# A one-core decoder block in float32: shared squares of x, a shorter sum of h, a second operand of w_o in halves, and a residual that is added in PSUM

## The reference

```
h      = rmsnorm(x, attn_norm_g)
proj   = h @ w_in            # conv B, C, x (1024 each), q 1024, k 128, v 128, two gates (1024 each)
y_conv = (u_b * short_conv(u_c * u_x)) @ w_conv_out          # causal, 3 taps
attn   = softmax over a window of 128 keys, with a position bias and a sink logit per head
mixed  = sigmoid(g_conv) * y_conv + sigmoid(g_attn) * (attn @ w_attn_out)
x      = x + mixed @ w_o
x      = x + square(relu(rmsnorm(x, mlp_norm_g) @ w_up)) @ w_down      # hidden 4096
out    = rmsnorm(x, final_norm_g)
```

## Time and profile before

| | us |
|---|---|
| median of 3 runs | 751.18 |
| the profiled execution | 751.2 |
| its span in the trace | 749.5 |
| PE busy (matmuls) | 741.1 (99%) |
| DVE busy | 656.3 (88%) |
| ACT busy | 430.0 (57%) |
| POOL busy | 85.5 (11%) |

### The profile page before, as it was taken

One profiled execution on the slowest core, in us unless ns is written; L12 is line 12 of the kernel. 1 busy time (PEld: TensorE's weight loads), 2 busy tenths in 40 slices (PEclk: granted clock), 3 DMA queues, 4 the chain that ended last, 5 costly groups with the idle time before them and its releaser, 6 DMA issues.

```text
span 749.5 us, 10670 instructions
## 1 busy us (share of the span) xinstructions
PE 741.1 (99%) x4198; PEld 650.7 (87%) x4198; DVE 656.3 (88%) x759; ACT 430.0 (57%) x551; POOL 85.5 (11%) x120
## 2 busy tenths in 40 slices
PE   9999999999999999999999999999999999999996
PEld 8899888888888888888888899889988999899985
DVE  5996788989899686989999999998799879986997
ACT  6773555453644557564658776654565455545555
POOL 1520000111122101010100101010101010100102
PEclk9999999999999999999999999999999999999999
DMA  9899313161247987777767747677677767686703
GB/s 319 200 316 321 112 57 113 57 164 61 84 127 236 305 232 196 195 225 193 255 169 177 213 124 208 179 201 193 169 191 202 174 171 219 168 215 180 197 1 113
DMA packets 69443, 135.45 MB, mean 181 GB/s; under 512 B 2636, under 2 KB 18068, under 8 KB 69396
## 3 DMA queue, kind: packets, MB, share of 16 engines
q1 hardware_dynamic: 48848, 85.23, 33.6%
q0 software_dynamic: 20336, 49.30, 30.3%
q10 hardware_dynamic: 212, 0.28, 0.1%
HBM read 128.48 MB, written 6.32 MB: 180 GB/s over the span
## 4 chain that ended last, share of the span: by engine, by line
PE 94%; DVE 4%; ACT 1%; issue 1%; POOL 0%; POOLq 0%; DVEq 0%; ACTq 0%
PE pair L1085 45%; PE pair L1044 22%; PE pair L790 6%; PE pair L792 6%; PE pair L791 6%; PE pair L911 3%; PE pair L837 2%; PE pair L812 1%; PE pair L811 1%; PE pair L821 1%; PE pair L859 1%; DVE h L1788 1%; PE pair L1007 0%; PE pair L995 0%; DVE wgt L1745 0%
## 5 line engine op out<-in xcount | busy, mean ns | idle before, releaser
L1390 ACT ACTIVATE high<-home_raw 128x2048 fp32r<-128x2048 f32 x91 | 174.3, 1916 | 148.4 <-PE pair L1085 102.9
L2014 DVE TENSOR_TENSOR home_lo<-home_raw,high 128x2048 fp32r<-128x2048 f32 x91 | 208.4, 2290 | 34.6 <-ACT high L1390 34.1
L1085 PE MATMUL pair<-high,s_hi_tile 128*128 128x512 f32 x440 | 110.3, 391 | 0.3 <-ACT s_hi_tile L1472 0.3
L1085 PE MATMUL pair<-high,s_lo_tile 128*128 128x512 f32 x440 | 109.9, 390 | 0.0
L1085 PE MATMUL pair<-home_lo,s_hi_tile 128*128 128x512 f32 x440 | 109.5, 389 | 0.0
L1085 PEld LDWEIGHTS pair<-home_lo,s_hi_tile 128*128 128x128 f32 x440 | 82.5, 188 | 17.1
L1085 PEld LDWEIGHTS pair<-high,s_lo_tile 128*128 128x128 f32 x440 | 82.4, 188 | 17.1
L1085 PEld LDWEIGHTS pair<-high,s_hi_tile 128*128 128x128 f32 x440 | 81.8, 188 | 17.7 <-issue 0.7
L790 PE MATMUL pair<-h,wgt 128*128 128x512 f32 x192 | 76.5, 399 | 0.0
L792 PE MATMUL pair<-h,wgt 128*128 128x512 f32 x192 | 75.0, 390 | 0.0
L791 PE MATMUL pair<-h,wgt 128*128 128x512 f32 x192 | 74.9, 390 | 0.0
(11 more groups left out here) (228 smaller groups left out, 1129.5 us busy)
## 6 DMA issues: line engine op xcount, KB each, us to landing
home_raw<-in_w_up SPq DMA_DIRECT2D x16, 1024.0 KB, 5.3
home_raw<-in_w_down SPq DMA_DIRECT2D x16, 1024.0 KB, 5.1
raw<-in_w_in SPq DMA_DIRECT2D x26, 512.0 KB, 4.8
home_raw<-in_w_up POOLq DMA_DIRECT2D x12, 1024.0 KB, 8.2
home_raw<-in_w_down POOLq DMA_DIRECT2D x12, 1024.0 KB, 8.4
home_raw<-in_w_in POOLq DMA_DIRECT2D x7, 1024.0 KB, 8.6
home_raw<-in_w_in SPq DMA_DIRECT2D x7, 1024.0 KB, 7.1
home_raw<-in_w_conv_out SPq DMA_DIRECT2D x4, 1024.0 KB, 5.2
```

Of the source, the lines that this page charges most:

```text
L1085: last = mm(pair[region(s, i)][:, b, :], a_[:, k, b * P:(b + 1) * P], w[:, k, :], start=(fresh and kind == 0 and k == 0), stop=(kind == 2 ...
L1390: a(high[n % 2][:, :], home_raw[home_of(s, name)][:, :], ACT.Copy).then_inc(m_hi, 1)
L2014: v.tensor_tensor(home_lo[home][:, :], home_raw[home][:, :], f32(high[n % 2][:, :]), ALU.subtract).then_inc(m_lo, 1)
```

## The change

Four places are touched.

**Squares of x.** For rows 0, ACT squares columns 0 to 511 only, and for rows 1 columns 0 to 767; DVE does the rest by a multiply with accumulation (`share_of_squares`), which leaves sum/1024 + 1e-6 in `share`. The root takes `share` as its bias instead of the constant. Both DVE pieces stand ahead of both `scale_x` on DVE, and rows 1 are scaled ahead of the copy of the parameters (`pcol`). On ACT `root(2)` moves ahead of the four copies of h's tiles.

**One h sum.** S1 = h11 + S2, computed in two steps from the split parts, becomes A - B from the two unsplit blocks in `qa`: one DVE instruction of 128 x 1024 for two. `hs_step` has one step fewer, and the copies that overwrite `qa` wait for step 4 instead of 3.

**w_o's second operand in halves.** ACT's high copy for N2 of stage WO becomes two of 128 x 512; TensorE's first two matmuls wait for the first (`o_first`), the third for the second.

**Last rows' residual in PSUM.** Ahead of the last product, DVE adds `res` of rows 3 into the accumulator in PSUM (`add_residual`), and TensorE waits for it (`rested`) before N4. The last `drain_n4` goes; ACT sums the squares and DVE scales straight from PSUM.

```diff
+SQUARED = (D // 2, 3 * D // 4, D, D)
...
+                            if s == WO and i == N2:
+                                pe.wait_ge(o_first, 1)
+                            elif s >= CO:
...
+                        if s == WO and i == N2 and (b, kind, k) == (0, 0, 2):
+                            pe.wait_ge(s_hi, part_no(s, i) + 1)
...
                 pe.wait_ge(drained, base_ + 4 + more)
+                if s == STAGES - 1:
+                    pe.wait_ge(rested, 1)
...
                 act.wait_ge(x_in[b], 16)
-                a(ta[:, :, :].rearrange("p a n -> p (a n)"), xn[:, b, :], ACT.Square,
+                n = SQUARED[b]
+                a(ta[:, :, :].rearrange("p a n -> p (a n)")[:, 0:n], xn[:, b, 0:n], ACT.Square,
                   accum_out=ssq[:, b:b + 1]).then_inc(sq_done, 1)
                 act.wait_ge(sq_done, b + 1)
-                a(rms[:, 0, b:b + 1], ssq[:, b:b + 1], ACT.Sqrt, bias=eps[:, :], scale=1.0 / D).then_inc(root_done, 1)
+                if n < D:
+                    act.wait_ge(share_done, b + 1)
+                a(rms[:, 0, b:b + 1], ssq[:, b:b + 1], ACT.Sqrt, bias=share[:, b:b + 1] if n < D else eps[:, :],
+                  scale=1.0 / D).then_inc(root_done, 1)
...
             q_high_half(M1, 1)
+            root(2)
             act.wait_ge(par_ready, 1)
...
-            root(2)
             q_high_half(N2, 0)
...
-                act.wait_ge(hs_step, {M7: 2, M6: 3, M5: 5, M3: 7}[i])
+                act.wait_ge(hs_step, {M7: 2, M6: 3, M5: 4, M3: 6}[i])
...
+                if (s, i) == (WO, N2):
+                    first = 2
+                    a(s_hi_tile[slot_of(s, i)][:, 0:2, :], src[:, 0:2, :], ACT.Copy).then_inc(o_first, 1)
+                a(s_hi_tile[slot_of(s, i)][:, first:4, :], src[:, first:4, :], ACT.Copy).then_inc(s_hi, 1)
...
-                act.wait_ge(drained, drained_before(STAGES - 1) + 6 + b)
+                if b < 3:
+                    act.wait_ge(drained, drained_before(STAGES - 1) + 6 + b)
+                else:
+                    wait_used(act, STAGES - 1, N4)
...
+            def share_of_squares(b):
+
+                n = D - SQUARED[b]
+                dve.wait_ge(x_in[b], 16)
+                v.tensor_tensor_reduce(out=ty[:, b, 0:n], in0=xn[:, b, D - n:D], in1=xn[:, b, D - n:D], scale=1.0 / D,
+                                       scalar=EPS, op0=ALU.mult, op1=ALU.add, accum_out=share[:, b:b + 1]
+                                       ).then_inc(share_done, 1)
...
+            share_of_squares(0)
+            share_of_squares(1)
             scale_x(0)
+            scale_x(1)
             dve.wait_ge(par_t, 1)
             v.tensor_copy(pcol[:, :], bank[KT - 1][:, T - 5 * KT:T]).then_inc(par_ready, 1)
-            scale_x(1)
...
             def h_s1():
-                step_done(3)
-                v.tensor_tensor(hs_sum[2][:, :, :], h_part(0, 0, 0), hs_sum[1][:, :, :], ALU.add).then_inc(hs_step, 1)
-                step_done(4)
-                v.tensor_tensor(hs_sum[2][:, :, :], hs_sum[2][:, :, :], h_part(1, 0, 0), ALU.add).then_inc(hs_step, 1)
+                v.tensor_tensor(hs_sum[2][:, :, :], four_of(qa, 1, 0), four_of(qa, 1, 1), ALU.subtract).then_inc(hs_step, 1)
...
+            def add_residual():
+
+                s = STAGES - 1
+                dve.wait_ge(drained, drained_before(s) + 5)
+                acc = pair[region(s, N4)][:, 1, :]
+                v.tensor_tensor(acc, acc, res[:, 3, 0:512], ALU.add).then_inc(rested, 1)
...
+                src = pair[region(STAGES - 1, N4)][:, 1, :] if b == 3 else r
...
                 if last:
+                    add_residual()
                     drain_last_m3(0)
...
             gain(3)
-            drain_n4(STAGES - 1, 1)
             factor(2)
```

More of the change, by code:

```diff
@@ L319, in build @@
         ssq = place("ssq", [P, TB])
+        share = place("share", [P, 2])
         rms = place("rms", [P, 2, TB])
@@ L364, in build @@
         h_hi, h_ready = sem("h_hi"), sem("h_ready")
-        wide = sem("wide")
+        wide, share_done = sem("wide"), sem("share_done")
         q_b11, q_b21 = ([sem(f"{n}{e}") for e in range(2)] for n in ("q_b11_", "q_b21_"))
@@ L393, in build @@
         copied, half_copied = sem("copied"), sem("half_copied")
-        o_seeded = sem("o_seeded")
+        o_seeded, o_first = sem("o_seeded"), sem("o_first")
         summed, relu_done = sem("summed"), sem("relu_done")
@@ L397, in build @@
         ao_sum = sem("ao_sum")
-        prod, drained, gfin_in = sem("prod"), sem("drained"), sem("gfin_in")
+        prod, drained, rested, gfin_in = sem("prod"), sem("drained"), sem("rested"), sem("gfin_in")
         passed = sem("passed")
@@ L1073, in product @@
                             pe.wait_ge(m_hi, n + 1)
-                            if s >= CO:
+                            if s == WO and i == N2:
+                                pe.wait_ge(o_first, 1)
+                            elif s >= CO:
                                 pe.wait_ge(s_hi, part_no(s, i) + 1)
@@ L1309, in q_copy @@
                 if i:
-                    act.wait_ge(hs_step, 3)
+                    act.wait_ge(hs_step, 4)
                 a(four_of(qa, i, j), four(Q_REGION.get(of, 3))[:, :, :], ACT.Copy, scale=scale).then_inc(done, 1)
@@ L1470, in s_high @@
                 wait_used(act, *part_before(s, i))
-                src = four(0) if (s, i) == (WO, N2) else part_source(s, i)
-                a(s_hi_tile[slot_of(s, i)][:, :, :], src[:, :, :], ACT.Copy).then_inc(s_hi, 1)
+                src, first = four(0) if (s, i) == (WO, N2) else part_source(s, i), 0
+                if (s, i) == (WO, N2):
+                    first = 2
+                    a(s_hi_tile[slot_of(s, i)][:, 0:2, :], src[:, 0:2, :], ACT.Copy).then_inc(o_first, 1)
+                a(s_hi_tile[slot_of(s, i)][:, first:4, :], src[:, first:4, :], ACT.Copy).then_inc(s_hi, 1)
             def seed(s):
@@ L1611, in square, with last_rows @@
                 a(a_part(s, i, j), src[:, :, :], ACT.Square).then_inc(squared, 1)
+            def last_rows(b, ch):
+                return pair[region(STAGES - 1, N4)][:, 1, :] if (b, ch) == (3, 0) else res[:, b, 512 * ch:512 * ch + 512]
             def sum_squares(b, ch, part):
-                a(tz[:, 0, 0:512], res[:, b, 512 * ch:512 * ch + 512], ACT.Square,
+                src = last_rows(b, ch) if part else res[:, b, 512 * ch:512 * ch + 512]
+                a(tz[:, 0, 0:512], src, ACT.Square,
                   accum_out=ss3[:, part, b:b + 1]).then_inc(ss3_ready, 1)
@@ L1846, in h_s4 @@
                 v.tensor_tensor(hs_sum[3][:, :, :], h_part(0, 0, 1), hs_sum[1][:, :, :], ALU.add).then_inc(hs_step, 1)
-                step_done(6)
+                step_done(5)
                 v.tensor_tensor(hs_sum[3][:, :, :], hs_sum[3][:, :, :], h_part(1, 0, 1), ALU.add).then_inc(hs_step, 1)
@@ L2375, in scale_late @@
                 r = res[:, b, 512 * ch:512 * ch + 512]
-                v.scalar_tensor_tensor(out=r, in0=r, scalar=rms3[:, 2, b:b + 1], in1=gfin[:, 512 * ch:512 * ch + 512],
+                src = pair[region(STAGES - 1, N4)][:, 1, :] if b == 3 else r
+                v.scalar_tensor_tensor(out=r, in0=src, scalar=rms3[:, 2, b:b + 1], in1=gfin[:, 512 * ch:512 * ch + 512],
                                        op0=ALU.mult, op1=ALU.mult).then_inc(out_late, 1)
```

## The result

The changed kernel takes 754.32 us, the median of 17 runs (749.62 to 756.28); the kernel before took 751.3 beside it. The ratio is 1.0033, with a 95% interval of 1.002 to 1.0046: slower by more than the 0.2% that can be told, where I had forecast 750.8 us and at most 751.2. The profiled execution took 755.48 us, with a span of 753.7 where the kernel before had 749.5. It is among the four longest: its mean granted clock is 0.993 of full speed, as in one other execution, where ten of the 17 have 0.997 and five 0.999 or more. What it lost by the clock is therefore at the upper end.

What follows compares the result with a forecast made beforehand. TensorE was taken as the bound, busy 741.1 of 749.5 us. Head -0.25, w_o 0.22 and end 0.44 summed to 0.41 us off 751.2, giving 750.8 us; own range 750.4 to 751.1, 80% range 749.6 to 751.2.

Steps and rivals of the forecast that it cites:

- The start: At the kernel's start, TensorE's idle 0.3 us before x's second rows goes: gain 0.3 us (bounds 0.15 to 0.4).
- The h sum: At M6's third kind, one DVE instruction fewer removes TensorE's wait for q's low part: gain 0.47 us.
- What holds these 0.8 us up: Before the first scores, a later bias table holds up the gains made so far, leaving -0.25 us.
- The bias table: Before the first scores, POOL's earlier 1 MB load delays the table from 68.46 to 69.3, scores to 72.50 us.
- the head: Everything up to the first scores: gains of 0.77 us are held up there, taken as -0.25 us.
- w_o: At stage WO, TensorE starts sooner on a halved operand until DVE's low part binds: gain 0.22 us (bounds 0.1 to 0.45).
- The end: Behind TensorE's last matmul, DVE's dropped add brings the last reciprocal forward: gain 0.44 us (bounds 0.2 to 0.5).
- The sum: Over the whole kernel, -0.25 + 0.22 + 0.44 = 0.41 us off, 750.8 us; chance 50%.
- rival A: Before the first scores, the bias table does not move: 1.16 us gained in all, 750.0 us; chance 20%.
- rival B: Before the first scores, the table lands 0.3 us or more earlier, no hold-up: 1.5 us gained, 749.7 us; chance 15%.
- Rival C: At the first scores, a 1.0 us TensorE wait drops the clock to 1.2 GHz, costing 2.6 us: 753.4 us; chance 3%.

Runs made afterwards that it cites:

- the repaired kernel: Changed kernel, with GpSimd also waiting for the landing of M5's data that SyncE waits for before issuing N4's load: 750.02 us, ratio 0.9982.
- the start alone: Kernel before with only the split squares of x's first rows and the scaling moved with it: 751.02 us, ratio 0.9996.
- the 24 transposes in the changed kernel: Changed kernel with 24 identity transposes, result unused, on TensorE ahead of product M3: 753.32 us, ratio 1.0027.
- fixed the wrong way: Changed kernel, with SyncE issuing M3's load only after a VectorE sum as well, so always behind N4's load: 755.02 us, ratio 1.0055.
- the end alone: Kernel before with only the last rows' residual added in PSUM ahead of the last product: 750.99 us, ratio 0.9998.
- all but the h sum: Changed kernel with the old two-step S1 computation put back: 750.12 us, ratio 0.9989.
- order alone in before: Kernel before with one added wait, so SyncE issues M3's load after GpSimd's load for N4: 752.84 us, ratio 1.0016.
- the h sum alone: Kernel before with only the one-instruction S1 from the unsplit blocks and its renumbered waits: 753.66 us, ratio 1.0037.
- the same, N4 not accumulating: Changed kernel with M3's load always behind N4's, and N4's load overwriting instead of accumulating, so it computes something else: 754.75 us, ratio 1.0043.

## Why the prediction was wrong, step by step

**The start** was right within its bounds, and the nearness of its number is in part luck. TensorE's first matmul of q came at 9.53 instead of 9.85 in the changed kernel, 0.32 us, with 0.3 forecast; in the repaired one it came at 9.66, 0.19. What the change gives is the stretch from the first transposes of x to that matmul: 2.24 and 2.25 us instead of 2.50, so 0.25. The rest is the 25 transposes of the identity, which took 5.19 us in the one execution and 5.60 in the other and in the kernel before.

**The h sum** was right for TensorE. Its third kind of M6 follows the second with no wait, in the repaired kernel after 1.91 us (36.08 to 37.99), worth 0.47 us: TensorE was 0.25 ahead at M6's first kind (34.41 to 34.16) and 0.72 at the group behind its third (40.63 to 39.91). It was incomplete: I took the low part of M6's weights as something for which TensorE alone waits.

**"What holds these 0.8 us up" is the step that failed,** and the rest of the error follows from it. It says that SyncE's loads "began when a DMA had landed (at 37.8), not when TensorE got somewhere", and that "the other queue does move". Both hold. But of GpSimd's queue it followed the stores and the load at 62.15 alone and left out the load for N4, which stands between the stores, hangs on VectorE's low part, and was issued 0.99 us behind SyncE's. With the h sum it was issued 1.65 us earlier (38.86 to 37.21), past a load that stayed where the landing put it: 37.9 in the profile of before, 38.7 to 39.0 in most of the others. What the runs showed in place of this step is a late landing of M3's weights (51.8 instead of 45.0), 2.34 us of start lost to TensorE's wait of 2.57, and 2.64 us at the lower clock; the sum had all three at nothing. The text bounded what a shift of one queue does to the bias table only; I had not listed the loads that lie behind the edit in both queues, nor asked who reads each.

**The bias table,** which was to take 0.25 us of the head, took nothing. In the repaired kernel it came 1.1 us earlier (67.37), though I had it land 0.8 later. GpSimd's load, said to move from 62.15 to 61.3, moved to 62.79. Where it did come earlier (61.63 with the start alone, 60.20 with the 24 transposes in the changed kernel), the table landed at 67.5, also earlier than 68.46. Its own issue was 0.71 us earlier in the repaired kernel (45.87 for 46.58) and 0.13 with the start alone, so the claim that an earlier issue gains nothing was not borne out either; why the table came 0.9 us earlier for 0.13 stays open. The scores moved from 72.27 to 71.71, and DVE's last operation for them ended at 67.96 + 2.47 = 70.43, 1.3 us ahead: neither the table nor the low part limited them. Of the 0.8 us of the head 0.56 were there: 0.72 up to M6's end, and 0.14 of it was lost ahead of M3 (0.58 at 51.92).

**w_o:** 0.22 us forecast. In the repaired kernel TensorE is 0.56 us ahead at the scores and 742.27 - 741.52 = 0.75 at its last group, so w_o gave 0.19. Beyond the head's 0.56 its first kind came 0.42 earlier and its third 0.31, and the third then took 1.95 us instead of 1.82 to the next group, which leaves 0.18: the restart behind VectorE's low part that the forecast took off, 0.13 instead of 0.09.

**The end:** 0.44 us forecast, 0.54 measured (2.98 to 2.44 us). The added operation was to push VectorE's queue by 0.14; the weights' low part at 737.00 came at 736.31 in the repaired kernel, 0.69 earlier where TensorE was 0.75 earlier, so it was pushed by 0.06.

**The sum** without the swap is 0.56 + 0.19 + 0.54 = 1.29 us; the repaired kernel's span is 1.3 shorter (748.2). My forecast of 0.41 would have been wrong there too, on the fast side: by its size that was rival A (1.16 us, 750.0), by its mechanism rival B (the table lands earlier and nothing holds the head up). **Rival C** had the right mechanism, a wait and then the lower clock, but at the scores, where no such wait came up; I gave it 3%, because I had looked for waits that the change makes at one place alone. Its price of 2.6 us against 2.64 in the profile of the changed kernel is luck: with the order fixed the wrong way it was 1.36. The Trainium skill (TensorE: Matmul & The Clock Gate, Part 1) has the clock taken back when idle. The traces with waits of 2.57, 2.67 and 2.75 us agree; the waits of 1.33 and 1.6 us left it at 2.4 GHz.

**What stays open.** Why the load that starts second gets its first packet only 2.2 to 4.6 us behind its issue, when SyncE's otherwise had one 1.0 to 1.4 us behind it (2.0 once), was not settled, only that accumulation is not the cause. Nor was it settled why the landing on which SyncE waits comes anywhere between 35.8 and 39.8 from one execution to the next. That the four shortest executions of the changed kernel are those in which it came early was not seen in a profile of that kernel; it is argued from the kernel with 24 transposes, whose profile had it.

## What to carry to other kernels

When an instruction comes earlier, list everything that waits for it, issues of DMAs first, and set each of those issues beside the issues of the other queues: an order that only the timing kept is lost without any wait or line changing. Where two loads must keep their order, give the second one the first one's condition; it cost nothing that could be seen here and made this change a gain of 1.25 us. And where a forecast has a wait of TensorE, look for a lower clock behind it: here waits of 2.57 and 2.67 us were followed by 2.64 and 1.36 us of it, and waits of 1.33 and 1.6 us by none.

## What was not expected of the hardware

A queue with 1 MB to load got no packet in 4 us (39 to 43) while another queue's load of the same size, issued 1.59 us earlier, had all the engines. The Trainium skill (DMA: Bandwidth & Descriptors, Queues, rings and completion order) has each engine go round-robin between the queues that it has work for, packet by packet. At 66 to 68 us that fitted nearly, and here it fits from 44 us on (128 packets each to 46); from 39 to 43 SyncE's queue got nothing, and whether the engines had work from it yet is not visible in the trace.

The kernel before has the same picture with the places changed. Its M3 load had its first packet at 39.23, and N4's load, issued at 38.86, began in earnest at 42.7. It had it a second time: GpSimd's load of 1 MB issued at 62.15 got no packet up to 65, while SyncE's queue had all the engines, and from 67 to 69 the two had nearly the same number (146 and 152). My prediction had read this start "some 3.4 us after issue" and used it for the bias table alone. So the load that starts second pays twice: it begins late, and then takes turns. M3's load is nearly through before the taking of turns begins only if it starts first.

| Kernel | N4's load leads by, us | M3's first packet behind its issue | M3's weights landed | TensorE's wait before M3 |
|---|---|---|---|---|
| before | -0.99 | 1.36 | 45.0 | none |
| N4 ordered behind | -0.47 | 1.00 | 44.1 | none |
| the end alone | 0.17 | 1.04 | 45.0 | none |
| all but the h sum | 0.41 | 1.05 | 44.7 | none |
| order alone in before | 1.04 | 2.21 | 51.7 | 1.33 |
| the h sum alone | 1.26 | 2.74 | 50.9 | 1.6 |
| the change | 1.59 | 4.35 | 51.8 | 2.57 |
| fixed the wrong way | 2.07 | 4.56 | 52.6 | 2.67 |
| the same, N4 not accumulating | 2.09 | 4.55 | 52.7 | 2.75 |

Between leads of 0.41 and 1.04 us the landing jumps by 7.0 us. The traces give a reason for the place of the jump. Where N4's load went first, its packets began 2.0 to 2.2 us behind its issue (39.24 for 37.21, 40.94 for 38.90); where M3's went first, its own began 1.0 to 1.4 us behind, and 2.0 in the profile with the 24 transposes. So by an estimate from these numbers, N4's packets come first once its issue leads by more than some 1.0 us. What decides is whose packets start first, and a lead of 0.17 or 0.41 us in issue did no harm.

The clock fell behind the waits of 2.57, 2.67 and 2.75 us, not behind those of 1.33 and 1.6. It cost 2.64, 1.36 and, by the same reckoning on the third trace (two groups of 2.76 and 2.63 us instead of 1.99 and 1.92), 1.48 us.
